# Projection into the state space: input split without the norm's scale in the gated layer, scale put on the results by VectorE

## The reference

```python
gate = jax.nn.sigmoid(rmsnorm(h, g_ple[i]) @ w_pg[i])
h = h + (p[i] @ w_pe[i]) * gate          # the gated layer
return rmsnorm(h, g_final)               # end of the first block

h = rms_norm(x, ssm_norm[i])             # start of the second block
u = h @ w_in                             # projection into the state space, 1024 x 1024
```

## Time and profile before

| | us |
|---|---|
| median of 3 runs | 2965.24 |
| lowest, highest | 2963.65, 2967.74 |
| the profiled execution, its span | 2966.1 |
| PE busy | 2631.9 (89%) |
| DVE busy | 1948.1 (66%) |
| POOL busy | 1676.7 (57%) |
| ACT busy | 822.5 (28%) |

### The profile page before, as it was taken

One profiled execution on the slowest core, in us unless ns is written; L12 is line 12 of the kernel. 1 busy time (PEld: TensorE's weight loads), 2 busy tenths in 40 slices (PEclk: granted clock), 3 DMA queues, 4 the chain that ended last, 5 costly groups with the idle time before them and its releaser, 6 DMA issues.

```text
span 2966.1 us, 32442 instructions
## 1 busy us (share of the span) xinstructions
PE 2631.9 (89%) x9809; PEld 1213.2 (41%) x9809; DVE 1948.1 (66%) x3967; ACT 822.5 (28%) x1792; POOL 1676.7 (57%) x1024
## 2 busy tenths in 40 slices
PE   7989888888887888878787989999999988999999
PEld 3454333333333333333333774444444434444444
DVE  7947777777777777777878673566335685566523
ACT  2423222222222222222233551222112245222101
POOL 5544444444444444544445857777776641677776
PEclk9999999999999999999998979999999998999999
DMA  4259999999999999999962323233332310233322
GB/s 139 67 202 416 421 422 421 416 408 421 415 419 412 410 410 419 415 413 402 422 248 60 95 58 102 92 99 107 111 97 86 120 59 8 72 105 99 121 96 82
DMA packets 133098, 696.15 MB, mean 235 GB/s; under 512 B 29867, under 2 KB 31180, under 8 KB 67052
## 3 DMA queue, kind: packets, MB, share of 16 engines
q0 software_dynamic: 73728, 536.90, 43.9%
q1 hardware_dynamic: 59244, 157.74, 16.4%
HBM read 686.72 MB, written 7.86 MB: 234 GB/s over the span
## 4 chain that ended last, share of the span: by engine, by line
PE 31%; DMA 25%; POOLq 16%; DVE 14%; issue 8%; ACT 3%; DVEq 2%; POOL 1%; ACTq 0%; SPq 0%
DMA R<-expert_uv_dram,idx 25%; PE bank L555 19%; POOLq L2604 8%; PE bank L769 8%; POOLq L2602 7%; DVE R L2044 3%; DVE Z L2066 1%; POOL R L2629 1%; DVE xt L2328 1%; ACT Z L1336 1%; DVE R L1789 1%; PE bank L1090 1%; DVE R L2436 1%; DVE R L2056 0%; DVE ci L1990 0%
## 5 line engine op out<-in xcount | busy, mean ns | idle before, releaser
L769 PE MATMUL bank<-R,Z 128*128 128x512 f32 x2048 | 968.8, 618 | 231.7 <-ACT Z L1336 227.3
L2629 POOL DMA_INDIRECT R<-expert_uv_dram,idx x512 | 596.0, 1164 | 722.5 <-PE bank L769 671.4
L555 PE MATMUL bank<-R 128*128 128x512 f16 (+1 forms) x4320 | 955.3, 382 | 14.6 <-DVE R L1773 7.0
L2044 DVE SCALAR_TENSOR_TENSOR R<-R 128x1024 f32<-128x1024 f32 x512 | 622.8, 1222 | 198.6 <-DMA R<-expert_uv_dram,idx 196.1
L769 PEld LDWEIGHTS bank<-R,Z 128*128 128x128 f32 x2048 | 381.1, 195 | 802.7 <-issue 415.4
L2601 POOL TENSOR_TENSOR R<-wring,beat 128x1024 f16<-128x1024 f32 (+2 forms) x223 | 456.8, 2048 | 427.1 <-PE bank L555 379.7
L555 PEld LDWEIGHTS bank<-R 128*128 128x128 f16 (+1 forms) x4320 | 420.5, 98 | 547.8 <-issue 33.8
L2603 POOL TENSOR_TENSOR R<-wring,R 128x1024 bf16<-128x1024 f32 (+2 forms) x223 | 520.3, 2333 | 32.4 <-issue 0.3
L1336 ACT ACTIVATE Z<-consts,R 128x128 f32<-128x128 f32 x512 | 177.6, 394 | 321.7 <-DVE R L2056 321.7
L555 PE MATMUL bank<-Z,R 128*128 128x512 f16 x1104 | 239.9, 379 | 1.5 <-POOLq L2604 1.5
L1329 ACT ACTIVATE R<-R 128x2 f32<-128x2 f32 x256 | 52.1, 203 | 606.1 <-DVEq L2046 605.8
(11 more groups left out here) (356 smaller groups left out, 2467.5 us busy)
## 6 DMA issues: line engine op xcount, KB each, us to landing
wring<-up_dram SPq DMA_DIRECT2D x88, 512.0 KB, 3.5
wring<-down_dram SPq DMA_DIRECT2D x32, 704.0 KB, 4.0
wring<-ple_dram SPq DMA_DIRECT2D x16, 640.0 KB, 3.8
wring<-w_in_dram SPq DMA_DIRECT2D x18, 512.0 KB, 3.5
R<-expert_uv_dram,idx POOLq DMA_INDIRECT x512
wring<-glu_dram SPq DMA_DIRECT2D x16, 512.0 KB, 3.6
Z<-w_q_dram SPq DMA_DIRECT2D x11, 512.0 KB, 8.0
wring<-ple_a_dram SPq DMA_DIRECT2D x8, 640.0 KB, 6.0
```

Of the source, the lines that this page charges most:

```text
L555: mm = pe.matmul(bank[:, :], low(w) if i else w, low(v) if j else v, start=(start and c == 0 and p == 0), stop=(stop and c == n - 1 and p ...
L769: mm = pe.matmul(banks[2 * par + c][:, :], diag[:, k % 4, :], pairs[:, slot, 1, c * SEQ:(c + 1) * SEQ], start=(k == 0), stop=(k == TOPK - 1))
L2044: dot = ve.scalar_tensor_tensor(pairs[:, slot, 0, :], pairs[:, slot, 0, :], 1.0, ntok[:, T, :], ALU.mult, ALU.mult, accum_out=act[:, par, ...
L2629: po.indirect_dma_start(pairs[:, slot, :, :].rearrange("p a b -> p (a b)"), None, A["expert_uv"], bass.IndirectOffsetOnAxis(idx[:, n % 2, ...
```

## The change

- The stage `ssm_in` no longer uses `norm_tiles`. In the gated layer ACT makes the high part of hT * `both_gains` (without a scale), and DVE the low part (`input_low`) one turn later, into the same `xs`.
- PE does tiles 0 to 4 of slab 0 ahead of the row sums and 5 to 7 behind them, then slab 1, then both spreads, then slabs 2 to 7.
- ACT copies `scale_bank` to `S_row`. DVE brings the results out (`chunk_tile`: bank times S_row, into the other order of tokens), among the operations of the tables; the last one stands in the middle of the final norm's eight operations.
- Of the tables, three operations go from DVE to ACT (AIs, Cm, shifts), `powers_ready` counts to three, and the sines come first on ACT. In `ssm` ACT starts when the last product is done.

```diff
@@ tensor
             if stage("final_a"):
+                s0, t0 = SLAB0["ssm_in"], TILE0["ssm_in"]
+                bank = banks[t0 % NBANK]
+                pe.wait_ge(split_done, used(s0))
+                free_bank(t0, 0, 0)
+                product(bank, s0 % NSPLIT, 0, 5, xs, a_ready, KT * SCALED.index("ssm_in"), stop=False)
                 pe.wait_ge(ss_ready, NORM["final_a"] + 1)
                 row_means(sumsq, stat_bank)
                 row_means(sumsq2, tile_banks[1])
-                norm_spread(NORM["ssm_in"], inv_both, scale_bank)
-                norm_spread(NORM["ssm_in"], inv, stat_bank)
+                product(bank, s0 % NSPLIT, 0, 3, xs, a_ready, KT * SCALED.index("ssm_in") + 5, start=False, first_of_slab=False, order=(5, 6, 7))\
+                    .then_inc(mm_done, 1)
                 finished(pe)
             if stage("ssm_in"):
-                plain("ssm_in", xs, a_ready, KT * SCALED.index("ssm_in"))
+                for i in range(1, SLABS["ssm_in"]):
+                    pe.wait_ge(split_done, used(s0 + i))
+                    free_bank(t0 + i, 0, 0)
+                    product(banks[(t0 + i) % NBANK], (s0 + i) % NSPLIT, 0, KT, xs).then_inc(mm_done, 1)
+                    if i == 1:
+                        norm_spread(NORM["ssm_in"], inv_both, scale_bank)
+                        norm_spread(NORM["ssm_in"], inv, stat_bank)
@@ scalar, in the loop of the gated layer
                         square(then, n)
+                        if then == "final_a":
+                            ac.activation(xs[:, n, 0, :], hT[:, n, :], ACT.Copy, scale=both_gains[:, n:n + 1])\
+                              .then_inc(hi_done, 1)
@@ scalar
             if stage("ssm_in"):
-                high_parts("ssm_in", xs)
-                for n in range(KT):
...
-                    ac.wait_ge(mm_done, used(t))
-                    ac.activation(uperm[:, n, :].rearrange("p (s j) -> p j s", j=NCH),
-                                  banks[t % NBANK][:, :].rearrange("p (j s) -> p j s", s=CH), ACT.Copy)\
-                      .then_inc(evac_done, 1)
...
+                ac.wait_ge(rb_mm, NORM["final_a"] + 1)
+                ac.activation(S_row, scale_bank[:, :], ACT.Copy).then_inc(s_ready, 1)
+                ac.activation(AI, bigP, ACT.Sin)
+                ac.activation(AR, bigP, ACT.Abs)
...
+                ac.activation(row(AIs), row(AI), ACT.Copy, scale=sgn)
+                ac.drain().then_inc(powers_ready, 1)
+                ac.activation(row(Cm), row(Cm), ACT.Copy, scale=nsgn[:, :])
+                ac.activation(shifts[:, 0:P], ident, ACT.Copy)
+                ac.drain().then_inc(powers_ready, 1)
@@ scalar, ssm
+                ac.wait_ge(mm_done, used(TILE0["ssm_in"] + KT - 1))
                 sines(0)
@@ vector
+            def input_low(k):
+                ve.wait_ge(hi_done, KT * len(TILED) + k + 1)
+                ve.scalar_tensor_tensor(low(xs[:, k, 1, :]), hT[:, k, :], both_gains[:, k:k + 1], xs[:, k, 0, :],
+                                        ALU.mult, ALU.subtract).then_inc(a_ready, 1)
@@ vector, gated: behind gather_square(then, n - 1) and ahead of angle_step(n); also at the end for KT - 1
+                        if then == "final_a":
+                            input_low(n - 1)
@@ vector, ssm_in
-                norm_tiles("ssm_in", lambda k: both_gains[:, k:k + 1], xs, a_ready)
...
+                def chunk_tile(n):
+                    t = TILE0["ssm_in"] + n
+                    ve.wait_ge(mm_done, used(t))
+                    ve.tensor_tensor(uperm[:, n, :].rearrange("p (s j) -> p j s", j=NCH),
+                                     banks[t % NBANK][:, :].rearrange("p (j s) -> p j s", s=CH),
+                                     S_row.rearrange("p (j s) -> p j s", s=CH), ALU.mult).then_inc(evac_done, 1)
+                angles(0)
+                ve.wait_ge(s_ready, S_READY["ssm_in"])
+                chunk_tile(0)
+                chunk_tile(1)
                 ve.wait_ge(prep, 3)
...
+                for n in range(NBANK, KT - 1):
+                    chunk_tile(n)
+                ve.wait_ge(rb_mm, NORM["ssm_in"] + 1)
                 for k in range(KT):
+                    if k == KT // 2:
+                        chunk_tile(KT - 1)
                     final = ve.scalar_tensor_tensor(hT[:, k, :], hT[:, k, :], col("g_final", k), stat_bank[:, :],
                                                     ALU.mult, ALU.mult)
@@ gpsimd
-                    po.wait_ge(powers_ready, 1)
+                    po.wait_ge(powers_ready, 3)
```

More of the change, by code:

```diff
@@ L192, in build @@
         SQUARES = [name for name in ("mixer", "peer", "final_a", "up0", "ple0", "attn", "up1", "ple1") if name in NORM]
-        TILED = [name for name in ("mixer", "ssm_in") if name in NORM]
+        TILED = [name for name in ("mixer",) if name in NORM]
         out_stored = sem("out_stored")
@@ L1493, in _ @@
             if stage("ssm_in"):
-                if not stage("final_a"):
-                    norm_root(NORM["ssm_in"])
-                high_parts("ssm_in", xs)
-                for n in range(KT):
[L1498 to L1506, removed]
-                    ac.wait_ge(mm_done, used(t))
-                    ac.activation(uperm[:, n, :].rearrange("p (s j) -> p j s", j=NCH),
-                                  banks[t % NBANK][:, :].rearrange("p (j s) -> p j s", s=CH), ACT.Copy)\
-                      .then_inc(evac_done, 1)
-                    if n == 1 and stage("ssm"):
-                        ac.wait_ge(ph_ready, 1)
-                        ac.activation(cosT[:, 0, :], ph_bank[:, :], ACT.Abs)
-                        ac.drain()
-                        ac.activation(cosT[:, 0, :], cosT[:, 0, :], ACT.Sin, bias=halfpi[:, :], scale=-TWO_PI)
@@ new lines, in _ @@
+                ac.wait_ge(rb_mm, NORM["final_a"] + 1)
+                ac.activation(S_row, scale_bank[:, :], ACT.Copy).then_inc(s_ready, 1)
+                ac.activation(AI, bigP, ACT.Sin)
+                ac.activation(AR, bigP, ACT.Abs)
+                ac.drain()
+                ac.activation(AR, AR, ACT.Sin, bias=halfpi[:, :], scale=-1.0)
+                ac.activation(lam_bank, row(spar[:, 0:2, :]), ACT.Copy)
+                ac.drain().then_inc(prep, 1)
+                ac.wait_ge(ph_ready, 1)
@@ new lines, in _ @@
+                ac.activation(cosT[:, 0, :], ph_bank[:, :], ACT.Abs)
+                ac.drain()
+                ac.activation(cosT[:, 0, :], cosT[:, 0, :], ACT.Sin, bias=halfpi[:, :], scale=-TWO_PI)
+                ac.wait_ge(prep, 4)
+                ac.activation(row(AIs), row(AI), ACT.Copy, scale=sgn)
+                ac.drain().then_inc(powers_ready, 1)
+                ac.activation(row(Cm), row(Cm), ACT.Copy, scale=nsgn[:, :])
+                ac.activation(shifts[:, 0:P], ident, ACT.Copy)
@@ L2279, in gated @@
                         gain_low(then, KT - 1)
+                    if then == "final_a":
+                        input_low(KT - 1)
             def ple(name, gains, then):
@@ L2382, in _ @@
                 ve.drain()
-                ve.tensor_scalar(row(AIs), row(AI), sgn, None, ALU.mult)
                 ve.tensor_tensor(den, den, prod_bank, ALU.add)
@@ L2399, in _ @@
                 ve.drain()
+                chunk_tile(2)
                 mul(bigP, each(fi_bank, GC), bbp)
@@ L2404, in _ @@
                 mul(bbp, each(fr_bank, GC), bbp)
-                ve.tensor_scalar(row(Cm), row(Cm), nsgn[:, :], None, ALU.mult)
+                chunk_tile(3)
                 ve.drain()
```

14 lines of the change are left out of this document (3 added, 11 removed).

## The result

The changed kernel takes 2976.84 us in the median of 6 runs (2974.89 to 2981.54), the kernel before 2967.48 in 6 runs beside it (2963.65 to 2968.16). The ratio is 1.0037, with an interval of 1.0027 to 1.0048: slower, by 9.4 us. The forecast was 2972.7 with a range of 2958 to 2979. The profiled execution after has a span of 2979.8, 13.7 more than before.

The account below looks back on a forecast made before the run. It took DVE, blocked by POOL's splits, to bound the gated layer and PE the projections: 18.1 us lost less 10.6 gained is +7.5, giving 2972.7 us, with a range of 2958 to 2979.

Parts of the forecast that it names:

- Which limit: Gated layer: not PE but DVE, busy for 80 to 91% of each turn, has no spare time; in the projections, PE.
- What is held up: Gated layer: an SBUF-to-SBUF operation on DVE waits for the running POOL operation's end, then runs its own length.
- The turns: Gated layer, turns 1 to 7 with blocking: 69.4 us against 51.4, so the last sum ends 18.1 us later.
- ACT's high parts at nothing: Gated layer: ACT's eight high parts of 0.706 us cost nothing, save 0.1 us in turn 1.
- The projection: From the row sums to the first transposes: 49.0 us in place of 59.6, so 10.6 us less.
- nine matmuls: Projection, rest of slab 0 behind the row sums: 3.5 us at low clock, 2.0 at full clock.
- the last result: End of the projection: bringing out the last result takes 1.1 us, and 0.1 to PE.
- the waits for splits: Projection, last six slabs: PE stands 1.8 us for splits, six sevenths of the earlier 2.1 us.
- The tables: State space tables behind the projection: ready at T + 38.3 against T + 41, slack about 3 us, so no cost.
- Rival D: Projection: DVE's large SBUF operations meet POOL's splits, tables late; up to 4 us on top of the forecast, 2976.7; chance 0.13.
- B: Gated layer: the low part blocks but displaces nothing, angle operations keep their times; +2.6 us, 2967.8; chance 0.19.
- C: Gated layer: low parts find POOL idle and cost 0.66 us each; -6.0 us, 2959.2; chance 0.18.

Follow-up runs that it names:

- e1: Changed kernel, but DVE's low part reads ACT's float32 copy in PSUM and one SBUF tile; median of 12 runs 2966.33 us, ratio 0.9998 to the kernel before.
- e7: The kernel of e1 again, unaltered, for another profile; one run 2971.73 us.
- e6: The kernel of e1 with eight one-element memsets added to DVE's list at the projection's end; median of 11 runs 2962.07 us, ratio 0.9983 to the kernel before.
- e4: Changed kernel without the angle operations of turns 3 to 5 (four left out); profiled span 2956.1 us, gated layer 63.20 us.
- e11: The kernel of e1 with each turn's angle operation right behind the addition into hT, one large one a turn; median 2957.08 us, ratio 0.9958 to the kernel before.
- e8: The kernel before, unchanged, profiled again; 2968.55 us, span 2966.7 us.
- the second execution: The changed kernel again, unaltered, for a second profile; 2976.43 us, span 2974.6 us.

## Why the prediction was right, and where it was off

**Which limit.** Right. DVE's order against POOL's splits decides, not PE: with the lock on the low part gone, the gated layer loses 16.5, 11.7 and 10.5 of the 18.8 us in three executions (e1, e7, e6).

**What is held up.** My reading of L2216 was right in its effect, but that row is a TENSOR_SCALAR and reads one SBUF tile, not two. It says nothing on operations with two SBUF inputs; for these stand L2243 in the earlier trace rows and the low parts after, 1.80 to 3.13 us in turns 1 to 6 and 0.75 behind them. Both forms are held up here: after, L2225 is a TENSOR_SCALAR too and takes 3.09 us. What they share is that all their operands lie in SBUF.

**The turns.** Laid out as 13.6, 11.2, 9.5, 10.8, 9.1, 8.9 and 6.3; they are 13.60, 11.19, 10.09, 10.83, 9.28, 8.92 and 6.42. Only turn 3 is off. I took POOL's start as 0.52 us behind PE's first matmul; at the low clock it was 0.73 (1568.54 to 1569.27), and the next turn began with a pause of 0.43. The start of the row sums was forecast at 1610.8 and came at 1611.03; since this execution began the layer 0.57 us earlier, that is 18.8 us more for the layer against 18.1.

**ACT's high parts at nothing.** Right: ACT is busy for 2.47 us in a turn of 9 to 11.

**The projection.** 49.0 forecast, 46.75 measured. By terms, forecast and measured: row sums 3.6 and 3.50; nine matmuls 3.5 and 2.54; slab 1 5.2 and 5.27; spreads 2.3 and 1.98; slabs 2 to 7 with their waits 33.2 and 32.22; the last result 1.2 and 1.24. Two terms were mis-sized. For the nine matmuls I took the low clock of the earlier trace rows; the granted clock was 0.50 in the row sums, but 0.93 in these 2.54 us, and they took 0.253 us each, near the 0.218 of full clock, though PE had stood for 8.85 us before the sums. And I scaled the waits for splits, 2.1 us, from the earlier trace rows, which was a misreading: of the 2.14 us that PE stood in that window only 1.07 were for splits (0.79 ahead of 1624.70, 0.28 ahead of 1635.51), and the other 1.07 were its end, the wait for the last result, which my sum has once more as a term of its own. After, PE waited for splits twice, 0.58 together. A result takes DVE 1.06, as taken from ACT's.

**The tables.** Slack forecast about 3 us; the last memset ended at 1647.06 and POOL began its products at 1651.27, so 4.2. Rival D did not happen; that the measured 2976.84 lies on its 2976.7 is chance. The last result and POOL's third product end together, so the first transposes are released by POOL (L2725).

**The rivals.** B, a block that displaces nothing, is refuted by the angle operations themselves: those of turns 3 to 6 take 2.24, 0.68, 1.23, 1.75 and 0.69 us before, and 3.09, 3.10, 1.23, 3.14 and 2.61 after. e4 agrees: four operations of 3.8 us gave 13.7. C, low parts that find POOL idle, is refuted by their median of 2.101. But its point of decision was real: who starts first. The kernel before already shows it: the L2220 of the earlier trace rows starts 0.27 us ahead of POOL's half (1574.59), takes its own 1.23, and the half takes 3.14 instead of 2.32. Where the order was set for it (e11), the gated layer is 57.37 us, against 58.09 before.

**The sum.** For this stretch I forecast 18.1 - 10.6 = +7.5; it is 18.8 - 12.8 = +6.0. The runs show +9.4. Two steps were off. The projection was forecast 2.3 us too long, mostly by the two terms above. And a step that I didn't write failed, that the layers behind keep their times. They don't: attention +3.3, the feed-forward layers ahead of it -1.6. For the stretch I was 1.5 us too high, for what lies behind it 1.7 too low, and that the two cancel is luck. Of the +9.4 between the medians these rows explain +7.7 and the 0.4 of the state space layer; the last 1.3 are open, and whether some of the six runs have the long state space layer no run shows. With them the second execution closes: 6.1 for the stretch, 0.4 for the state space layer, 1.7 behind, 0.4 for a later start, 8.6 against 8.5 between the spans 2974.6 and 2966.1. In the first profile the long state space layer adds 6.2 more. Of the miss of 4.1 us in the time itself, 1.9 is +9.4 against +7.5, and the other 2.2 is the base: the three runs shown had a median of 2965.24, the six have 2967.48. The profiled executions took 1.7 to 1.9 us more than their spans (2968.55 for 2966.7 in e8), where I had put the run 0.9 below.

## What to carry to other kernels

When work with all its operands in SBUF goes to VectorE beside GpSimd's running operations (in the gated layer TENSOR_TENSOR, SCALAR_TENSOR_TENSOR and TENSOR_SCALAR were held up; the sums and low parts with an input in PSUM were not: 0.68 to 0.69 us each), don't add up its own length: lay out one turn with both engines and see whom it pushes over whose next operation, for here 0.7 us of work took 2.1 and made most turns 3.1 to 4.6 us longer. What helps is one input in PSUM, or such an operation placed directly behind the event that will release GpSimd, so that it starts first; GpSimd then paid 0.85 us in e11 and 1.01 in e1. And a kernel whose order is decided by a few hundredths of a microsecond can differ by 5 us in that stage between two executions: compare several profiled executions of it before explaining a median.

## What the runs showed of the hardware that I had not expected

- The same stage of the same program has two lengths, 107.0 and 113.2 us. In the long one the granted clock stays at 1.2 GHz for 24 us in a row, nearly all of it with PE at work; in the short one the slow stretches come in pieces, with nearly the same sum. What decides it is open.
- Eight tiny instructions on VectorE, over 600 us ahead, shorten attention by 3.1 us. That they do so by moving the pauses of 0.43 and 0.68 us in its instruction list is argued from their places, not shown.
- Being first is enough, for the angle operation L2232: 0.07 us ahead gave DVE its 1.23 us, 0.69 us behind cost it 3.18.
